# A diffusion trunk layer on one core: merge products with split operands and early loads, paired doubling steps in the scan

## The reference

```python
mod = silu(cond) @ w_ada + b_ada            # sh1, sc1, g1, sh2, sc2, g2
h = x * (1.0 + sc1) + sh1
proj = h @ w_in                             # Fourier part, r/k/v, lora parts, two gates
o_f = fourier_mix(u_f) @ w_fo               # 512 -> 1024
y = scan(forward) + scan(backward)          # RWKV-7: 16 heads of 64, state 64x64 a head
o_r = (norm(y) * g) @ w_ro                  # 1024 -> 1024
mix = (sigmoid(gate_f) * o_f + sigmoid(gate_r) * o_r) @ w_out
x = LN(ALPHA * x + g1 * mix)
h2 = x * (1.0 + sc2) + sh2
x = LN(ALPHA * x + g2 * expert_choice_ffn(h2))   # softmax, top_k per expert, 16 experts
```

## Time and profile before

| what | value |
|---|---|
| median of 3 runs | 2687.97 us (2686.44 to 2688.4) |
| the profiled execution: time / span | 2687.13 us / 2685.2 us |
| mean granted TensorE clock | 0.961 |
| PE busy | 2420.9 us (90%) |
| DVE / ACT / POOL busy | 984.9 / 615.4 / 363.8 us |
| DMA | 538.55 MB, 201 GB/s over the span |

### The profile page before, as it was taken

The page is one execution under the profiler, slowest core; times in us unless marked ns, Lnnn a source line. Parts: engine busy times, 40 slices in busy tenths (PEclk is TensorE's granted clock), DMA queues, the critical chain, the costliest instruction groups (busy, mean ns, idle before and its releaser), DMA issues. The chain is left out here.

```text
span 2685.2 us, 58051 instructions
## 1 busy us (share of the span) xinstructions
PE 2420.9 (90%) x26165; PEld 1504.4 (56%) x26165; DVE 984.9 (37%) x1737; ACT 615.4 (23%) x1179; POOL 363.8 (14%) x405
## 2 busy tenths in 40 slices
PE   5999996688998998999689949999999999999993
PEld 3999995577787787788445513333333333333331
DVE  3344311658468467475113431121212212121114
ACT  2122222435535445443200100111111111111111
POOL 0000000315315325224000600000000000000000
PEclk8999998799999999999889969999999999999997
DMA  8363331000000000000361179999999999999974
GB/s 339 102 242 103 112 112 60 19 20 5 26 25 5 27 25 5 26 8 5 126 238 43 71 291 401 400 394 392 396 396 395 396 394 382 399 396 395 395 294 162
DMA packets 180715, 538.55 MB, mean 201 GB/s; under 512 B 13254, under 2 KB 53926, under 8 KB 180216
## 3 DMA queue, kind: packets, MB, share of 16 engines
q1 hardware_dynamic: 177400, 524.39, 50.5%
q0 software_dynamic: 3072, 10.49, 1.8%
HBM read 504.15 MB, written 30.70 MB: 199 GB/s over the span
## 5 line engine op out<-in xcount | busy, mean ns | idle before, releaser
L1724 PE MATMUL ps_h_lat<-w_piece,xT 128*64 128x512 f32 x2048 | 456.7, 599 | 8.6 <-DVE hidden L1846 7.5
L1724 PEld LDWEIGHTS ps_h_lat<-w_piece,xT 128*64 128x64 f32 x2048 | 145.7, 138 | 312.9 <-issue 312.9
L1749 PE MATMUL ps_y_lat<-w_piece,hiddenT 128*64 128x512 f32 x1024 | 232.6, 596 | 0.9 <-ACT hiddenT L1610 0.9
L1733 PE MATMUL ps_h_ctx<-w_piece,xT 128*16 128x512 f32 x2048 | 226.1, 593 | 0.0
L1840 DVE TENSOR_TENSOR hidden<-sigmoid_lat,ps_h_lat 64x1024 f32<-64x1024 f32 x32 | 39.1, 1223 | 506.6 <-ACT sigmoid_ctx L1616 506.6
L325 PE MATMUL ps_in<-hT_hi,w_in_hi 128*128 128x320 f32 x752 | 173.3, 312 | 3.0 <-issue 3.0
L666 POOL TENSOR_TENSOR Mo<-x,levels_sb 128x256 f32<-128x256 f32 x200 | 161.9, 832 | 99.2 <-PE ps_scan L908 99.1
L325 PE MATMUL ps_in<-hT_lo,w_in_hi 128*128 128x320 f32 x752 | 172.0, 310 | 0.0
L325 PE MATMUL ps_in<-hT_hi,w_in_lo 128*128 128x320 f32 x752 | 172.0, 310 | 0.0
L908 PE MATMUL ps_scan<-TT_diag,Mo 64*64 64x64 f32 x3200 | 115.0, 220 | 43.8 <-issue 26.6
L1749 PEld LDWEIGHTS ps_y_lat<-w_piece,hiddenT 128*64 128x64 f32 x1024 | 70.2, 137 | 138.3 <-issue 137.7
(11 more groups left out here) (278 smaller groups left out, 3530.1 us busy)
## 6 DMA issues: line engine op xcount, KB each, us to landing
w_piece<-in_w_e SPq DMA_DIRECT2D x192, 2048.0 KB, 13.5
w_ada<-in_w_ada SPq DMA_DIRECT2D x6, 4096.0 KB, 17.8
w_in_raw<-in_w_in SPq DMA_DIRECT2D x23, 1024.0 KB, 6.3
rkv_scratch<-projected SPq DMA_DIRECT2D x24, 320.0 KB, 6.2
rkv_T<-rkv_scratch SPq DMA_DIRECT2D x8, 960.0 KB, 5.1
gates_scratch<-projected SPq DMA_DIRECT2D x16, 320.0 KB, 6.7
gate_sb<-gates_scratch SPq DMA_DIRECT2D x8, 640.0 KB, 6.3
x<-in_x_sample SPq DMA_DIRECT2D x8, 512.0 KB, 6.5
```

What stands on the lines that cost most here:

```text
L1724: last = pe.matmul(psA[rows, cs], x[:, k, A], w[:, q, cs], start=(k == 0), stop=(k == KD - 1))
L1733: last = pe.matmul(psB[GRP[g], :], x[:, k, B], w[:, q, c * 512:(c + 1) * 512], start=(k == 0), stop=(k == KD - 1))
L1749: last = pe.matmul(psY[rows, :], hT[:, f, A], w[:, q, c * 512:(c + 1) * 512], start=(hf == 0 and f == 0), stop=(hf == 1 and f == FK - 1))
```

## The change

What it does, phase by phase:

- Front: both first pieces of w_ada are loaded ahead of x, each in two halves with semaphores of their own; the bias is loaded by ScalarE's queue; modulation(1) writes another PSUM tile (wide[0]) and doesn't wait for the sum of modulation(0); all transposes of x come after the modulation.
- Scan: groups 0 and 1 are taken together in the z and T.Z steps, their products interleaved, and in group 1 (chunks 2 and 3, CROSSED) T and Z lie in the opposite half of the partitions, so that successive products fall in all four quarters of the array. For them 8 more products of 64x64 are made and evicted in each of two pair stages. The order of the rounds on TensorE, ScalarE and VectorE is new. fT and the first block of w_fo for the merge are loaded by SP in the first tile.
- Merge: fT, yg, w_fo and w_ro are split into high and low parts, and the products take the split form; the Fori loops are written out; w_out, w_router, x and the vectors are loaded behind the first blocks; yg comes in three parts; the last token tile's output products, its normalise and the top-k search are interleaved.
- Experts: the two constants are loaded in the merge.

```diff
@@ front_phase
             def load_ada(r):
-                sp.dma_start(w_ada[r % 2][:, :, :], wa_view[:, :, r * RW:(r + 1) * RW]).then_inc(s_wa[r % 2], 16)
+                for ks, landed in zip(KHALF, s_wa[r % 2]):
+                    sp.dma_start(w_ada[r % 2][:, ks, :], wa_view[:, ks, r * RW:(r + 1) * RW]).then_inc(landed, 16)
...
+            load_ada(0)
+            load_ada(1)
             for t in range(NT):
                 src = d["x_sample"][0, t * P:(t + 1) * P, :] if t < CT else d["x_prompt"][0]
                 sp.dma_start(x[:, t, :], src).then_inc(s_x[t], 16)
-            load_ada(0)
-            load_ada(1)
-            b_view = d["b_ada"].rearrange("a (r c n) -> (a c) r n", c=CP, n=CW)
-            for c in range(CP):
-                for j in range(2):
-                    sp.dma_start(bias[32 * c + j:32 * c + j + 1, :, :], b_view[c:c + 1, :, :]).then_inc(s_bias, 16)
...
             def modulation(r):
-                pe.wait_ge(s_wa[r % 2], 16 * (r // 2) + 16)
-                if r >= 1:
+                if r >= 2:
                     pe.wait_ge(s_mod, r)
                 for k in range(KD):
+                    if k % KHALF[1].start == 0:
+                        pe.wait_ge(s_wa[r % 2][k > 0], 16 * (r // 2) + 16)
...
-            for k in range(3):
-                turn_x(k)
             pe.wait_ge(s_ct, 1)
             modulation(0)
             modulation(1)
...
-            for k in range(3, KD):
+            for k in range(KD):
                 turn_x(k)
@@ scan_phase
+    CROSSED = (2, 3)
...
+            sp.dma_start(early[0][:, :, :], d["fT"]).then_inc(s_early, 16)
+            sp.dma_start(early[1][:, :, :], d["w_fo"][0].rearrange("(k p) n -> p k n", p=P)[:, :, 0:P]).then_inc(s_early, 16)
...
                     for h in range(2):
+                        if n in CROSSED:
+                            act.activation(T[:, n, h::2, :], b_m(h)[:, 5 * HD:7 * HD].rearrange("p (e n) -> p e n", e=2), ACT.Copy)
...
-                    evict(0)
-                    evict(1)
                     for b in range(NGR):
-                        if b == 1:
-                            evict(2)
+                        evict(b)
+                    for b in range(NGR):
                         if not last and PER_ROUND * rd + b < NSLOT:
                             front(PER_ROUND * rd + b, i + 1, 1 - m)
...
+                    if n in CROSSED:
+                        for x, xs in enumerate(HALVES):
+                            for h, hs in enumerate(HALVES):
+                                last = pe.matmul(b_m(h)[HALVES[1 - x], (5 + dr) * HD:(6 + dr) * HD], AR[m][dr][hs, g, 0, xs], B[dr][hs, at(x)],
+                                                 start=True, stop=True)
...
+            def problems(bs, l):
+
+                both = [[(b, c, p, q, x) for c, p in enumerate(range(*GROUPS[b])) for q in range(2 if l == TOP else NPROB) for x in range(2)]
+                        for b in bs]
+                return [one for pair in zip(*both) for one in pair]
...
+                for b, c, p, q, x in problems(bs, l):
                     if l < TOP:
+                        last = pe.matmul(ps_of(b_z(b), b)[HALVES[x ^ (p in CROSSED)], c, q, :], Mo[HALVES[x], p, q, :], TD[HALVES[x], p, q, :],
+                                         start=True, stop=True)
...
                 for rd in range(TOP):
-                    z_step(i, NGR * rd)
-                    z_step(i, NGR * rd + 1)
+                    z_step(i, rd, (0, 1))
+                    z_step(i, rd, (2,))
...
+                        slot(PER_ROUND * rd)
+                        tt_step(i, rd, (0, 1))
+                        dt_step(0)
+                        slot(PER_ROUND * rd + 1)
+                        dt_step(1)
+                        tt_step(i, rd, (2,))
+                        dt_step(2)
+                        slot(PER_ROUND * rd + 2)
...
+                    slot(PER_ROUND * rd)
+                    if rd < TOP - 1:
+                        add_tt(rd, 0)
+                        add_tt(rd, 1)
+                        add_t(rd, 0)
+                    slot(PER_ROUND * rd + 1)
+                    if rd < TOP - 1:
+                        add_t(rd, 1)
+                        add_tt(rd, 2)
+                        add_t(rd, 2)
+                    slot(PER_ROUND * rd + 2)
@@ merge_phase
+            load(0, 1)
+            for n, (k0, k1) in enumerate(Y_PARTS):
+                sp.dma_start(y_raw[:, k0:k1, :], d["yg"][:, k0:k1, :]).then_inc(s_in[n], 16)
+            load(1, 0)
+            load(1, 1)
...
+            for c in range(2, KD):
+                for n in range(2):
+                    sp.wait_ge(s_mm, 2 * (c - 2) + n + 1)
+                    load(c, n)
+                sp.wait_ge(s_mt, c - 1)
+                load_gates(c)
+                if c in (2, 3):
+                    half = slice((c - 2) * KD // 2, (c - 1) * KD // 2)
+                    sp.dma_start(w_out[:, half, :], wo_view[:, half, :]).then_inc(s_wo, 16)
...
+                    for k in range(kt):
+                        if c == 0:
+                            pe.wait_ge((s_flo, s_ylo)[n], k + 1)
+                        for p, (w, x) in enumerate(((whi, x_hi), (whi, x_lo), (wlo, x_hi))):
+                            for b in range(2):
+                                last = pe.matmul(acc[:, b * 512:b * 512 + HALF], w[:, k, :], x[:, k, b * HALF:(b + 1) * HALF],
+                                                 start=(k == 0 and p == 0), stop=(k == kt - 1 and p == 2))
...
+            out(CT, ((0, 0, KD),))
+            turn(CT - 2)
+            logits(CT - 3)
             turn(CT - 1)
             logits(CT - 2)
             logits(CT - 1)
+            out(CT, ((1, 0, KD // 2),))
+            affinities(0)
+            out(CT, ((1, KD // 2, KD),))
             turn(CT)
...
+            for t in range(CT):
+                normalise(t)
...
             softmax(0)
...
-            choose(0, LAT, CAP_L // 16)
+            choose(0, LAT, 3)
+            normalise(CT)
+            choose(0, LAT, 4)
             softmax(1)
-            choose(0, LAT, CAP_L // 16)
+            choose(0, LAT, 1)
@@ expert_phase
             def consts():
-                sp.dma_start(iota[:, :], d["iota_slot"]).then_inc(s_cst, 16)
-                sp.dma_start(tokid[:, :], d["tok_id"]).then_inc(s_cst, 16)
```

361 lines of the change are left out of this document (207 added, 154 removed).

## The result

| | before | after |
|---|---|---|
| median | 2688.18 us (2686.44 to 2688.77) | 2709.14 us (2701.64 to 2711.9, 4 runs) |
| profiled execution: time / span | 2687.13 / 2685.2 us | 2701.64 / 2699.8 us |
| mean granted TensorE clock | 0.961 | 0.928 |

The ratio is 1.0075, with a 95% interval of 1.0054 to 1.0096: the changed kernel is slower by some 20 us where 27 us less were forecast. All four runs of it are slower than all four of the kernel before. The front and the merge came as forecast. First their rows, from the timeline of the changed kernel: VectorE's bias sum, ScalarE's split of w_in and the first input product.

A forecast was written before the change was run, and what follows sets the result against it. It took TensorE to fill the input products, scan and merge, but VectorE to pace the scan's doubling rounds, and DMA the experts. Front -8, merge -41, merge end -2 and scan +24 gave -27: 2660 us, range 2632 to 2678.

The forecast's parts named there:

- Front, -8: Ahead of the first input product: reordered loads cover the bias wait, ScalarE's w_in split ends at 37.0; gain 8.2 us.
- Merge, -41: Merge: split products cut a block to 10.6 us, a load wait goes, the start is earlier; 19 + 12 + 10 us.
- the fourth rival: Merge keeps its period because loads or low parts pace it; 2691 us, chance 0.04.
- End of the merge and experts, -2: Around softmax and top-k search: copy one us earlier, constants' 0.9 us of SP issue saved; -2, between 0 and -4.
- Scan, +24: Scan: the new order's waits outweigh the pairing, +3.5 us a tile, seven times; bounds -8 to +48.
- The walk: Scan, one middle tile step by step: waits in rounds 0 to 4 put the full inverse at 1087.6, not 1084.6, +3 us.
- the third rival: Scan: quarters do not run together, products keep 58 ns, +8.8 us in all eight tiles; 2730 us, chance 0.04.
- the second: Scan: TensorE is the bound after all and takes what the pairs save; 2574 us, half of that 2605; chance 0.07.
- One of the prediction's own signs: Scan: a first paired z of 32 products in 1.1 us was to mean right, 1.8 us wrong.
- VectorE's list from the first prefix sum on: Scan: 43 to 44 us of work, starting no earlier than 1040.8, ending about as before; a tile gains at most 1 us.
- At most 2 us, half of it hidden: Scan: cost per tile of TensorE's clock halving after the 4 us gap at z of group 2.
- The rival that named the walk too harsh: Scan: ScalarE and VectorE overlap better than listed, scan comes out even; 2636 us, chance 0.20.

The follow-up runs named there:

- E6: Changed kernel with useless bf16 products where TensorE stands in round 0, ahead of later T.Z and z of group 2, and ahead of the chain; 2687.13 us.
- E8: Changed kernel with the old scan put back, but z of group 2 moved ahead of w_dec's products and T.Z of group 0 in round 0; 2665.68 us.
- E10: E7 without the pairs: no crossed products or evictions, products of groups 0 and 1 one group after the other; 2676.86 us.
- E7: Changed kernel, pairs kept, with the old order of steps on TensorE and ScalarE and the new order on VectorE; 2637.93 us.
- E13: E11 with ScalarE's third Z eviction also moved behind its first front job in round 0; 2664.76 us.
- E11: Changed kernel with z of group 2 moved behind T.Z of groups 0 and 1 and the first T update, in round 0 on TensorE alone; 2713.57 us.
- E12: Changed kernel, in round 0 w_dec's products ahead of z of group 2 and ScalarE's first sigmoid ahead of the third Z eviction; 2686.45 us.
- E9: E7 with useless bf16 products in TensorE's stops, ahead of the first paired z and ahead of the paired T.Z; 2632.67 us.
- E2: Changed kernel with useless bf16 products ahead of both z steps of round 0 and ahead of the paired T.Z of later rounds; 2707.76 us.

## Why the prediction was wrong

**Front, -8: right**, by its own steps. It said 37.0 for the end of w_in's split, and the row says 35.96 and 1.91 (37.9). The bias sum is at 29.24, and the first product at 47.12: the step from the split to it took 9.2 us for a forecast 10.0 and made up for the late 0.9.

**Merge, -41: right** in the sum and in both terms the rows can show, the period (10.56 for 10.6) and the wait that went. Over the eight blocks TensorE is busy 87.27 of 87.30 us. VectorE's low parts paced nothing, so the fourth rival is out.

**End of the merge and experts, -2: wrong by 3.5.** The rows are the copy for the top-k search and the slots' positions:

```profile
1548.68 0.68 DVE L1604 COPY top_work<-ps_merge 16x512 f32<-16x512 f32 x1 [5.29 <-PE ps_merge L1484]
...
1576.95 0.24 DVE L1623 COPY posT<-ps_merge 128x80 f32<-128x80 f32 x1 [0.81 <-PE ps_merge L1507]
1577.49 0.24 DVE L2001 COPY gate_tok<-tok_id_sb 128x5 f32<-128x5 f32 x2 [0.30 <-PEq L1289]
```

VectorE waited 5.29 us for the affinities, where 2.5 was forecast. With the normalise of 7.2 us in the middle of the search the slots stood 111.6 us after the last merge block (1576.95 - 1465.33), 108.7 before. Two of these 2.9 us came back in the next step, where the wait for the constants, 2.31 us, is gone; the forecast had counted 0.9 for it.

**Scan, +24: the step that failed.** It measured +62.4. The walk had the wait for z(2) right: it put z(2) at 1035.6, 23.5 us into the tile, and it came at 23.3, with ScalarE's sigmoids behind it. The quarters' pairing, 30 ns for a forecast 33, was right as well; the third rival is out, and so is the second, since the scan got longer. By the Trainium skill's rule on row tiles and a PSUM bank (TensorEngine Tiling (Array Packing), Restrictions and Gotchas), which the prediction weighed, the products would not have overlapped; the trace again differs, by those 30 ns. One of the prediction's own signs misleads here: the first paired z took 1.92 us, and 1.8 was to mean that the quarters don't run together. It ran at half clock; in E6, at full clock, the same products take 1.16 us.

Two sizes were off, both in the same direction.

- "VectorE's list from the first prefix sum on" was said to start 3.2 us late at the least and to end 1.6 late, because a sum is done ahead of it and GpSimd disturbs it less. It starts 5.1 us late and ends 5.3 late, a list of 44.7 for 44.5. The reason given was right, VectorE's work in it is 1.9 us less, but VectorE's waits for ScalarE took it back, and the walk gave them no time in the list. E8 shows the rule cleanest: start +3.6, tile +3.6.
- "At most 2 us, half of it hidden" for half clock, laid to z(2)'s stop alone. The two stops of round 0 gave 0.65 over 14.6 us, some 10 us at half clock, beginning with the stop ahead of the first paired z, which the walk didn't have. In four tiles of six the chain at the tile's end ran slow too, for 4.3 us, and that was nowhere in the sum. E6 prices both: with the clock held the start is 28.4 instead of 30.6, 2.9 late for the 3.2 of the walk, the chains are 29.7, and even with the fills' own 1.3 in the tail, the tile is 3.6 shorter.

Per tile: start +5.1 (2.2 of it the clock, by E6), list +0.2, tail +1.1 (1.4 forecast, for three groups in a row), chain +2.9 on average; 9.2 in six tiles where 3.5 was forecast, 6.1 in the first and 1.1 in the last.

The rival that named the walk too harsh had the sign wrong: it was too mild. The pairing's saving was real on TensorE (30 ns for 58, and PE busy 88.80 in the tile of 108.4, 92.74 before, half-clock stretches included) and could hardly be had, about 1 us a tile by E10, since TensorE did not bind the rounds. The change's loss is thus shown by E7 and E13 to be the place of a few steps, not what they compute. What decides whether a chain of the changed kernel falls to half clock or not was not settled: in the tile from 1044.0 the clock was full from 1114 to 1123, TensorE stood 1.8 us between 1119 and 1124, and the chain went slow at 1124.

## What to carry to other kernels

Look for the engine whose list fills a stage, then for the one instruction that starts that list, and follow what is queued ahead of it on every engine: here one eviction ahead of a sigmoid cost 49 us in a scan (E13 against E11). Making an engine faster that doesn't bind wins little, 1 us of 8.8 here, and joining steps makes each wait for the later of two inputs: the first paired z stood 2.45 us. Such stops can cost TensorE's clock in the work behind them. A kernel in which some chains run slow and some don't also spreads: 23 and 24 us from run to run in E10 and E12, 4 us in E6 and E9 with the clock held.

## What the runs showed of the hardware

- 22 us were won by adding some 107 products of no use a tile (2003 TensorE records against 1896): E6. Their places matter: E2, with none in rounds 2 to 5 ahead of z(2) and none added ahead of the chain, won nothing.
- The same five prefix sums on VectorE took 1.69, 2.78 and 3.97 us, the longer the more of GpSimd's work ran beside them.
- A stretch that is itself 95% busy can run at half clock: 46 TensorE records for 84 in 10 us of the chain, after 9 us at full clock. It was gone in E6, where the stops ahead of it were filled.
